# Dealing the modulation groups of a two-layer diffusion backbone out anew over the chunks of layer 0

## The chip, the cores and the metric

The kernel runs on one core of a Trainium2 chip. The metric is the device time of one execution in microseconds (us). The core has these engines: PE multiplies matrices, DVE (VectorE) and ACT (ScalarE) work on tensors, POOL (GpSimd) does a little of that too, and SP only issues transfers. Each engine works through its own queue in program order and waits on semaphores for the others.

## The reference, cut to what matters

Two layers work on 256 latent tokens and 256 context tokens of 1024 channels. Every layer begins with a modulation: a vector per stream (c for the latent tokens, c_ctx for the context) goes through silu and a 1024 x 6144 weight, and gives six vectors of 1024 (shift, scale and gate of the mixer, shift, scale and gate of the feed-forward part).

```python
def adaln(cvec, w, b):
    m = jax.nn.silu(cvec) @ w + b
    return [t[..., None, :] for t in jnp.split(m, 6, axis=-1)]

for l in range(DEPTH):
    sh1, sc1, gt1, sh2, sc2, gt2 = adaln(c, w_ada[l], b_ada[l])
    csh1, csc1, cgt1, csh2, csc2, cgt2 = adaln(c_ctx, w_ada[l], b_ada[l])
    hx = modulate(rms_norm(x, g_mix[l]), sh1, sc1)      # the same for ctx
    ...                                                 # four branches, merged, @ w_out
    x = x + gt1 * mixer_output(...)
    x = x + gt2 * conv_ffn(modulate(rms_norm(x, g_ffn[l]), sh2, sc2), w_up[l], ..., w_down[l])
```

In the last layer the context only gives keys and values, so of its modulation only shift and scale of the mixer are needed there.

## The kernel before

**Chunks.** All weights stream through in 244 chunks, 122 to a layer, each 128 x 1024 to 128 x 1408 numbers. The stages of a layer and their first chunk: in 0, fn 18, sc 26, at 34, cf 46, out 54, up0 62, dn0 84, up1 92, dn1 114. Layer 0 has both streams (512 columns for a matmul), layer 1 has one (256 columns). Numbers such as "chunk 72" below are of layer 0.

**Three products.** For every chunk ACT copies the raw weights to `w_hi` (`head`, L881), DVE subtracts to get `w_lo` (`rest`, L1165), and PE multiplies three times (L480 to L482). Both run AHEAD = 3 chunks in front of PE: in its step n the DVE first makes the rest of chunk n+3, then waits for PE to finish chunk n, reads its result out of PSUM (in the stages out and dn this is the residual, L1529, two instructions of 256 columns; in the up stages L1555 and L1558 for an even chunk and L1565 for an odd one), and last does `ada_behind`. PE begins a chunk when its rest is there and the chunk four before it has been read out.

**Lead.** At the start of out, up0 and dn0/dn1 PE computes the first three chunks together (`lead`), so it needs the rests of all three before it begins; their results come almost together.

**Norm.** After stage out and after dn1 comes a norm, and PE has nothing to multiply until its first channels are there. Its chain: DVE reads out the last chunk (of out: chunk 61, in two halves, one for each stream), ACT squares the half, PE sums, ACT takes the root, DVE the reciprocal (L1239) and a diagonal, PE spreads it, DVE scales (L1269), ACT adds the shift, DVE gives the remainder (L1280). During stage out DVE also adds the squares of the earlier chunks (`add_square`, L1234).

**Modulation groups.** The 12 groups of 1024 modulation values (layer 0: 0 to 5, layer 1: 6 to 11, in the order of the reference) take eight chunks of `w_ada` each. Groups 1 and 0 are done by PE at the start. For the other ten `ADA_START[g]` is the chunk of layer 0 behind which the first of eight steps is done, `ada_step`: DVE multiplies a 128 x 1024 piece of `w_ada` with a column of the silu and adds it to `ada_sum` (L1186; the first step of a group L1184). Groups 0 to 7 have two vectors (c and c_ctx) and take two such instructions a step; I call them double. Groups 8 to 11 are single. After the eighth step DVE folds `ada_sum` to 128 x 32 for each vector (L1193). `REDUCE` gives the chunk in front of which PE does the last reduction (`reduce_in_front`, L522), for which it waits for the folds; DVE reads it one step earlier in its own count (`read_mod`, L1205, L1214), since PE reduces behind chunk n-1 and in front of n.

**Transfers.** SP loads chunks and `w_ada` pieces into four shared slots of `raw`, in one fixed order (`FILLS`), each when the entry four before it has been used.

Of the kernel before, what the change touches and what calls it, by code (L numbers as in the profile page):

```python
# [15 lines left out]
ALU = mybir.AluOpType  # L16
ACT = mybir.ActivationFunctionType
AX = mybir.AxisListType
# [28 lines left out]
START, SIZE, LEN = {}, [], {}  # L47
# [10 lines left out]


ADA_START = {2: START["in"] + 2, 3: START["at"] + 3, 4: START["at"] + 11}  # L60
for _g in range(5, 12):
    ADA_START[_g] = START["up0"] + 8 * (_g - 5)
ORDER = [1, 0] + sorted(ADA_START, key=ADA_START.get)
POS = {_g: _p for _p, _g in enumerate(ORDER)}
REDUCE = {START["out"] + 3 if _g == 4 else ADA_START[_g] + 10: _g for _g in ADA_START}
ADA_AT = {ADA_START[_g] + _k: 8 * _g + _k for _g in ADA_START for _k in range(8)}
assert len(ADA_AT) == DEPTH * ADA_L - ADA_A and max(REDUCE) < PER_LAYER - 1
ADA_LOADS = [(0, 1), (1, 1)] + [(_i, 2) for _i in range(2, ADA_A, 2)]
# [13 lines left out]
def ada_vectors(a):  # L82


    return 2 if a < ADA_L or a % ADA_L < 16 else 1
# [69 lines left out]
def program(nc, io):  # L155
    ctx = ExitStack()
    with ctx:
# [23 lines left out]
        ada_sum = place("ada_sum", [2, KD * P])  # L181
# [31 lines left out]
        ada_part = place("ada_part", [2, P * KD // 32])  # L213
# [47 lines left out]
        csil_done, nsink_done, mod_done, gsc_done = map(sem, ("csil_done", "nsink_done", "mod_done", "gsc_done"))  # L261
# [895 lines left out]
        def _(dve):  # L1157
# [13 lines left out]
            def ada_step(a):  # L1171

                p, g, kk = PLACE[("ada", a)], a // 8, a % 8
                dve.wait_ge(raw_full[p % SLOTS], 16 * (p // SLOTS + 1))
                if kk == 0 and g == 2:
                    dve.wait_ge(reduced, 2)
                elif kk == 0:
                    dve.wait_ge(folded, POS[g] - 2)
                else:
                    dve.wait_ge(ada_acc, ADA_STEPS[a] - ada_vectors(a))  # L1180
                for vv in range(ada_vectors(a)):
                    w, dst, c = raw[:, p % SLOTS, 0:KD * P], ada_sum[:, vv, :], csil[:, kk, vv:vv + 1]
                    if kk == 0:
                        op = dve.tensor_scalar(dst, w, c, None, ALU.mult)  # L1184
                    else:
                        op = dve.scalar_tensor_tensor(dst, w, c, dst, ALU.mult, ALU.add)  # L1186
                    op.then_inc(ada_acc, 1)
                if kk == KD - 1:

                    dve.wait_ge(ada_acc, ADA_STEPS[a])  # L1190
                    dve.wait_ge(reduced, POS[g])
                    for vv in range(ada_vectors(a)):
                        op = dve.tensor_reduce(ada_part[:, vv, :], ada_sum[:, vv, :].rearrange("p (b k) -> p b k", k=32),  # L1193
                                               AX.X, ALU.add, apply_transpose=True)
                    op.then_inc(folded, 1)

            def read_mod(g, bank):

                dve.wait_ge(reduced, POS[g] + 1)
                layer, c0 = g // 6, KD * (g % 6)  # L1200
                b = VEC["b_ada"] + KD * g
                vs = ada_vectors(8 * g)
                ps = bank[:, 0:2 * KD].rearrange("p (c v) -> p v c" if g < 2 else "p (v c) -> p v c", v=2)
                for vv in range(vs):
                    op = dve.tensor_tensor(mod[:, layer, c0:c0 + KD, vv], ps[:, vv, :], vec[:, b:b + KD], ALU.add)  # L1205
                op.then_inc(mod_done, 1)
                if g % 6 in (1, 4):

                    dve.wait_ge(mod_done, POS[g] + 1)
                    which = g % 6 // 3  # L1210
                    gv = VEC["g_mix" if which == 0 else "g_ffn"] + KD * layer
                    for vv in range(2):
                        if vv < vs:
                            op = dve.scalar_tensor_tensor(gsc[:, which, vv, :], mod[:, layer, c0:c0 + KD, vv],  # L1214
                                                          1.0, vec[:, gv:gv + KD], ALU.add, ALU.mult)
                    op.then_inc(gsc_done, 1)

            def ada_behind(st):

                if st.i is None:  # L1220
                    if st.n + 1 in REDUCE:
                        read_mod(REDUCE[st.n + 1], psB[(st.n + 1) % 2])
                    if st.n in ADA_AT:
                        ada_step(ADA_AT[st.n])

# [26 lines left out]
            def norm(layer, which):  # L1252
                r = 2 * layer + which
                if r:
                    inverse_root(r, 0)
                dve.wait_ge(gsc_done, r + 1)
                for s in range(norm_streams(r)):
                    h0 = 16 * r + KD * s
                    cols = slice(s * SEQ, (s + 1) * SEQ)
                    dve.wait_ge(spread, normed(r, s))  # L1260
                    for kk in range(KD + 1):
                        if r == 2 and s == 1 and kk in SPLIT_IN_NORM:
                            if kk:
                                query(Step(PER_LAYER + SPLIT_IN_NORM[kk] - 1, SPLIT_IN_NORM[kk] - 1))
                            rest(Step(PER_LAYER + SPLIT_IN_NORM[kk], SPLIT_IN_NORM[kk]), SIZE[AHEAD])
                        if kk < KD:
                            if kk >= 2:
                                dve.wait_ge(h_rest, h0 + kk - 1)
                            dve.scalar_tensor_tensor(tmp[kk % 2][:, cols], X[:, kk, cols],  # L1269
                                                     gsc[:, which, s, kk:kk + 1], spread_bank[s][:, cols],  # L1270
                                                     ALU.mult, ALU.mult).then_inc(ht, 1)
                        if kk == 1 and s == 0:
                            if r == 0:
                                read_mod(ORDER[1], psB[1 + ORDER[1]])
                            if norm_streams(r) > 1:
                                inverse_root(r, 1)
                        if kk >= 1:
                            c = kk - 1
                            dve.wait_ge(h_head, h0 + c + 1)
                            dve.scalar_tensor_tensor(h_lo[:, c, cols], tmp[c % 2][:, cols],  # L1280
                                                     mod[:, layer, 24 * which + c, s:s + 1],
                                                     h_hi[:, c, cols].bitcast(F32), ALU.add, ALU.subtract)\
                                .then_inc(h_rest, 1)
# [8 lines left out]
            for ahead in range(AHEAD):  # L1292
                dve.wait_ge(ada_pe, first_free(2 * SLOTS + ahead))
                if ahead == AHEAD - 1:
                    g = ORDER[1]
# [4 lines left out]
            for layer in range(DEPTH):  # L1300
# [6 lines left out]
                for idx in range(LEN["in"]):  # L1307
                    st = Step(n0 + idx, idx)
# [41 lines left out]
                    if 6 <= idx < 11:  # L1350
# [3 lines left out]
                        r = 15 * layer + 3 * j  # L1354
# [104 lines left out]
                for idx in range(LEN["at"]):  # L1459
                    st = Step(m0 + idx, idx)  # L1460
# [243 lines left out]
```

## Time and profile before

| | us |
|---|---|
| median of 3 runs | 1343.0 (1340.77 to 1345.43) |
| profiled execution, own time | 1344.04 |
| its span | 1342.3 |
| PE busy | 1287.8 (96%) |
| DVE busy | 883.2 (66%) |
| ACT busy | 555.6 (41%) |
| POOL busy | 289.8 (22%) |

The span runs from the first to the last instruction of the profiled execution, and the time is 1.7 us longer than it. PE's granted clock was 0.985 of full speed on average. An engine's busy share says little of where it is late: what counts here are the few places at which PE stands still, and what it waits for there.

### The profile page before, as it was taken

The numbers are of one execution on the slowest core, as the hardware profiler recorded it, in microseconds if no ns is written. First come the engines' busy times: TensorE is split into PE (matmuls) and PEld (weight loads), VectorE is DVE, ScalarE is ACT, GpSimd is POOL, SyncE is SP. The second block draws the span as 40 slices with busy tenths as digits, with TensorE's granted clock in tenths as the row PEclk, the third lists the DMA queues.
The fourth block names the chain that finished last, engine by engine and source line by source line (L and its number), as shares of the span: only waits on it lengthen the run. The fifth ranks groups of instructions, "written<-read, shape, count | busy, mean of one in ns | idle before, by whom it ended". The sixth has DMA issues, their size and how long they took to land.

```text
span 1342.3 us, 19885 instructions
## 1 busy us (share of the span) xinstructions
PE 1287.8 (96%) x7677; PEld 1101.3 (82%) x7677; DVE 883.2 (66%) x1193; ACT 555.6 (41%) x868; POOL 289.8 (22%) x246
## 2 busy tenths in 40 slices
PE   7999999999999999999999999989999998999997
PEld 1788877777788788787788888889888898999997
DVE  1686378753689568997656664576677466764654
ACT  2322345654333234333123332344566464653543
POOL 0000499310223100112001110002782230120210
PEclk9899999999999999999999999989999999999999
DMA  9364221222546323667456663425333554564560
GB/s 371 112 188 153 81 76 61 71 63 63 161 141 247 107 82 121 202 195 223 140 166 193 196 204 122 151 79 173 119 118 98 169 174 142 172 214 147 181 211 32
DMA packets 51234, 198.75 MB, mean 148 GB/s; under 512 B 5584, under 2 KB 6864, under 8 KB 50896
## 3 DMA queue, kind: packets, MB, share of 16 engines
q1 hardware_dynamic: 51152, 197.62, 45.2%
q8 instruction: 56, 0.92, 0.3%
q14 instruction: 26, 0.21, 0.1%
HBM read 196.55 MB, written 1.05 MB: 147 GB/s over the span
## 4 chain that ended last, share of the span: by engine, by line
PE 78%; DVE 13%; issue 4%; ACT 3%; DMA 1%; SPq 0%; DVEq 0%; ACTq 0%
PE psA L480 22%; PE psA L482 22%; PE psA L481 22%; DVE w_lo L1165 3%; DVE ada_sum L1186 2%; DVE acc L1374 2%; PE psB L480 2%; PE psB L481 2%; PE psB L482 2%; ACT w_hi L881 1%; DMA ada_first<-w_ada 1%; PE psA L501 1%; DVE small L1387 1%; PE psB L726 1%; PE psB L633 1%
## 5 line engine op out<-in xcount | busy, mean ns | idle before, releaser
L480 PE MATMUL psA<-h_hi,w_hi 128*128 128x256 f32 (+1 forms) x1568 | 529.8, 338 | 9.5 <-DVE h_lo L1280 6.4
L481 PE MATMUL psA<-h_lo,w_hi 128*128 128x256 f32 (+1 forms) x1568 | 523.4, 334 | 0.0
L482 PE MATMUL psA<-h_hi,w_lo 128*128 128x256 f32 (+1 forms) x1568 | 523.3, 334 | 0.0
L881 ACT ACTIVATE w_hi<-raw 128x1024 fp32r<-128x1024 f32 (+2 forms) x244 | 277.1, 1138 | 340.3 <-PE psA L482 243.8
L1165 DVE TENSOR_TENSOR w_lo<-raw,w_hi 128x1024 fp32r<-128x1024 f32 (+2 forms) x244 | 332.7, 1364 | 126.7 <-ACT w_hi L881 126.5
L480 PEld LDWEIGHTS psA<-h_hi,w_hi 128*128 128x128 f32 x1568 | 302.6, 193 | 38.5 <-issue 7.6
L481 PEld LDWEIGHTS psA<-h_lo,w_hi 128*128 128x128 f32 x1568 | 302.7, 193 | 28.1 <-issue 0.5
L482 PEld LDWEIGHTS psA<-h_hi,w_lo 128*128 128x128 f32 x1568 | 302.2, 193 | 28.0
L469 POOL TENSOR_TENSOR hid_lo<-sig,hid_hi 128x512 f32 (+3 forms) x44 | 67.7, 1538 | 486.7 <-ACT hid_hi L1129 486.7
L1186 DVE SCALAR_TENSOR_TENSOR ada_sum<-raw,csil,ada_sum 128x1024 f32<-128x1024 f32 x112 | 159.3, 1452 | 0.0
L480 PE MATMUL psA<-hid_hi,w_hi 128*128 128x256 f32 (+1 forms) x352 | 117.8, 335 | 3.5 <-DVE sig L1565 2.1
L482 PE MATMUL psA<-hid_hi,w_lo 128*128 128x256 f32 (+1 forms) x352 | 117.3, 333 | 0.0
L481 PE MATMUL psA<-hid_lo,w_hi 128*128 128x256 f32 (+1 forms) x352 | 117.3, 333 | 0.0
L1529 DVE SCALAR_TENSOR_TENSOR X<-psA,mod,X 128x256 f32<-128x256 f32 x55 | 25.1, 479 | 85.7 <-PE psA L482 85.7
L480 PEld LDWEIGHTS psA<-hid_hi,w_hi 128*128 128x128 f32 x352 | 66.9, 190 | 11.0 <-DVE w_lo L1165 4.1
L444 POOL TENSOR_TENSOR acc<-acc,sqb 128x512 f32<-128x512 f32 (+1 forms) x60 | 74.5, 1241 | 5.0
L482 PEld LDWEIGHTS psA<-hid_hi,w_lo 128*128 128x128 f32 x352 | 66.9, 190 | 6.5
L481 PEld LDWEIGHTS psA<-hid_lo,w_hi 128*128 128x128 f32 x352 | 66.9, 190 | 6.4
L450 POOL TENSOR_TENSOR X<-X,tmp 128x512 f32<-128x512 f32 (+1 forms) x28 | 43.3, 1555 | 125.2 <-DVE tmp L1479 76.3
L1140 ACT ACTIVATE tmp<-psA,vec 128x512 f32<-128x512 f32 (+1 forms) x44 | 29.5, 671 | 96.2 <-PE psA L482 96.2
L1555 DVE SCALAR_TENSOR_TENSOR tmp<-psA,vec,tmp 128x510 f32<-128x510 f32 (+1 forms) x44 | 27.0, 613 | 62.1 <-ACT tmp L1140 62.0
L480 PE MATMUL psB<-y_hi,w_hi 128*128 128x512 f32 (+1 forms) x128 | 46.6, 364 | 13.4 <-issue 7.3
(170 smaller groups left out, 1453.9 us busy)
## 6 DMA issues: line engine op xcount, KB each, us to landing
raw<-w_up SPq DMA_DIRECT2D x88, 512.0 KB, 4.2
raw<-w_ada SPq DMA_DIRECT2D x80, 512.0 KB, 3.6
raw<-w_dn SPq DMA_DIRECT2D x32, 704.0 KB, 5.2
raw<-w_in SPq DMA_DIRECT2D x36, 512.0 KB, 4.3
raw<-w_at SPq DMA_DIRECT2D x24, 512.0 KB, 3.5
raw<-w_fn SPq DMA_DIRECT2D x16, 640.0 KB, 3.9
raw<-w_sc SPq DMA_DIRECT2D x16, 640.0 KB, 3.9
raw<-w_cf SPq DMA_DIRECT2D x16, 640.0 KB, 4.0
```

The lines of the kernel that those rows point to most:

```text
L444: pool.tensor_tensor(dst, dst, part, ALU.add).then_inc(tap_pool, 1)
L450: pool.tensor_tensor(dst, dst, src[:, 0:T], ALU.add).then_inc(m_sum, 1)
L469: pool.tensor_tensor(dst, sig[b][:, 0:T], src.bitcast(F32), ALU.subtract)\
L480: pe.matmul(out, w0, hi, start=first, stop=False)
L481: pe.matmul(out, w0, lo, start=False, stop=False)
L482: return pe.matmul(out, w1, hi, start=False, stop=last)
L881: act.activation(w_hi[:, s, 0:tiles * P], raw[:, r, 0:tiles * P], ACT.Copy).then_inc(head_done, 1)
L1140: act.activation(tmp[b][:, 0:T], psA[st.slot][:, 0:T], ACT.Identity, bias=Vd("ffn_b", st.up(p0 + pair, 2)), scale=Vd("ffn_w", st.up(3 * (p ...
L1165: dve.tensor_tensor(w_lo[:, s, 0:tiles * P], raw[:, r, 0:tiles * P], w_hi[:, s, 0:tiles * P].bitcast(F32), ALU.subtract).then_inc(rest_don ...
L1186: op = dve.scalar_tensor_tensor(dst, w, c, dst, ALU.mult, ALU.add)
L1374: op = dve.scalar_tensor_tensor(dst, src, w, dst, ALU.mult, ALU.add)
L1555: dve.scalar_tensor_tensor(t3[:, :, 1:SEQ], p3[:, :, 0:SEQ - 1], Vd("ffn_w", st.up(w, 6)), t3[:, :, 1:SEQ], ALU.mult, ALU.add).then_inc(cv, 1)
```

## The change

It alters at which chunks the groups 5 to 11 are done, and it separates the two folds of a double group.

| group | vectors | chunks before | reduced before | chunks after | reduced after |
|---|---|---|---|---|---|
| 2, 3, 4 | 2 | 2-9, 37-44, 45-52 | 12, 47, 57 | the same | the same |
| 5 | 2 | 62-69 | 72 | 53-60 | 65 |
| 6 | 2 | 70-77 | 80 | 84-91 | 94 |
| 7 | 2 | 78-85 | 88 | 108-115 | 118 |
| 8 | 1 | 86-93 | 96 | 62-69 | 72 |
| 9 | 1 | 94-101 | 104 | 70-77 | 80 |
| 10 | 1 | 102-109 | 112 | 92-99 | 102 |
| 11 | 1 | 110-117 | 120 | 100-107 | 110 |

So after the change no group is worked on behind chunks 61, 78 to 83 and 116 to 121. The first fold of a double group stays in the step of its eighth product. The second is done one step later, after that step's result has been read out and before that step's product, if there is one (`ADA_END`). The waits of the norms for their scale (`gsc_done`) get the counts of the new order (`GAINS`).

```diff
-for _g in range(5, 12):
-    ADA_START[_g] = START["up0"] + 8 * (_g - 5)
+for _g, _n in [(5, START["cf"] + 7), (8, START["up0"]), (9, START["up0"] + 8), (6, START["dn0"]), (10, START["up1"]),
+               (11, START["up1"] + 8), (7, START["up1"] + 16)]:
+    ADA_START[_g] = _n
 ORDER = [1, 0] + sorted(ADA_START, key=ADA_START.get)
 POS = {_g: _p for _p, _g in enumerate(ORDER)}
-REDUCE = {START["out"] + 3 if _g == 4 else ADA_START[_g] + 10: _g for _g in ADA_START}
+REDUCE = {{4: START["out"] + 3, 5: START["up0"] + 3}.get(_g, ADA_START[_g] + 10): _g for _g in ADA_START}
+ADA_END = {ADA_START[_g] + 8: _g for _g in ADA_START}
+GAINS = {_r: 1 + sum(ADA_START[_g] <= ADA_START[_h] for _g in (4, 7, 10)) for _r, _h in [(1, 4), (2, 7), (3, 10)]}
+GAINS[0], GAINS[3] = 1, max(GAINS[2], GAINS[3])
...
                     dve.wait_ge(ada_acc, ADA_STEPS[a])
                     dve.wait_ge(reduced, POS[g])
-                    for vv in range(ada_vectors(a)):
-                        op = dve.tensor_reduce(ada_part[:, vv, :], ada_sum[:, vv, :].rearrange("p (b k) -> p b k", k=32),
-                                               AX.X, ALU.add, apply_transpose=True)
+                    ada_fold(g, 0)
+
+            def ada_fold(g, vv):
+
+                op = dve.tensor_reduce(ada_part[:, vv, :], ada_sum[:, vv, :].rearrange("p (b k) -> p b k", k=32),
+                                       AX.X, ALU.add, apply_transpose=True)
+                if vv == ada_vectors(8 * g) - 1:
                     op.then_inc(folded, 1)
...
                     if st.n + 1 in REDUCE:
                         read_mod(REDUCE[st.n + 1], psB[(st.n + 1) % 2])
+                    if st.n in ADA_END and ada_vectors(8 * ADA_END[st.n]) == 2:
+                        ada_fold(ADA_END[st.n], 1)
                     if st.n in ADA_AT:
                         ada_step(ADA_AT[st.n])
...
-                dve.wait_ge(gsc_done, r + 1)
+                dve.wait_ge(gsc_done, GAINS[r])
```

## Rows read from the trace of the kernel before

**Rows 1.** The page: totals of the engines; loads of `w_ada`, us to landing.
```profile
PE 1287.8 (96%) x7677; PEld 1101.3 (82%) x7677; DVE 883.2 (66%) x1193; ACT 555.6 (41%) x868; POOL 289.8 (22%) x246
...
raw<-w_ada SPq DMA_DIRECT2D x80, 512.0 KB, 3.6
```

**Rows 2.** Timeline of PE: start us, us, what; in brackets the idle before, and its releaser.
```profile
447.35 0.47 PE L480 MATMUL psA<-mg_hi,w_hi 128*128 128x512 f32 x1 [1.62 <-DVE w_lo L1165]
...
557.40 0.26 PE L522 MATMUL psB<-ada_part,mat 128*32 128x16 f32 x8 [3.04 <-DVE ada_part L1193]
...
626.51 0.47 PE L480 MATMUL psA<-hid_hi,w_hi 128*128 128x512 f32 x1 [1.30 <-DVE w_lo L1165]
...
658.44 0.26 PE L522 MATMUL psB<-ada_part,mat 128*32 128x16 f32 x8 [1.73 <-DVE ada_part L1193]
```

**Rows 3.** Windows: length, busy us of PE, PEld, DVE, ACT, POOL, granted clock, DMA share, GB/s.
```profile
554.38:564.95 10.57, 7.55 (x33) 6.12 (x34) 10.50 (x14) 3.37 (x4) 1.23 (x1) 0.84 0.58 179
603.02:608.90 5.88, 5.88 (x33) 4.86 (x34) 5.88 (x8) 1.69 (x2) 1.63 (x1) 1.00 0.67 214
570.38:575.83 5.45, 5.45 (x25) 4.52 (x25) 5.45 (x5) 1.70 (x2) 1.49 (x1) 1.00 0.68 230
...
491.93:515.55 23.62, 20.96 (x163) 20.82 (x164) 17.04 (x40) 9.59 (x20) 0.00 (x0) 0.93 0.08 24
1131.99:1147.59 15.60, 12.19 (x80) 11.76 (x81) 9.46 (x21) 5.68 (x12) 0.00 (x0) 0.78 0.18 55
...
625.22:649.25 24.03, 22.74 (x100) 18.88 (x101) 7.83 (x8) 3.19 (x3) 1.61 (x1) 1.00 0.34 105
809.80:832.59 22.79, 22.70 (x100) 18.86 (x101) 5.08 (x6) 3.18 (x3) 1.60 (x1) 1.00 0.32 103
```

**Rows 4.** Timeline of DVE at the start of stage out.
```profile
462.64 0.88 DVE L1529 SCALAR_TENSOR_TENSOR X<-psA,mod,x_in 128x256 f32<-128x256 f32 x2 [10.13 <-PE psA L482]
463.79 1.23 DVE L1165 TENSOR_TENSOR w_lo<-raw,w_hi 128x1024 fp32r<-128x1024 f32 x1 [0.28 <-ACT w_hi L881]
464.93 0.87 DVE L1529 SCALAR_TENSOR_TENSOR X<-psA,mod,x_in 128x256 f32<-128x256 f32 x2
...
466.85 0.68 DVE L1234 TENSOR_TENSOR sqa<-sqa,sqb 128x512 f32<-128x512 f32 x1
467.45 0.87 DVE L1529 SCALAR_TENSOR_TENSOR X<-psA,mod,x_in 128x256 f32<-128x256 f32 x2
468.24 0.23 DVE L1205 TENSOR_TENSOR mod<-psB,vec 128x8 f32<-128x8 f32 x2
...
468.66 1.22 DVE L1165 TENSOR_TENSOR w_lo<-raw,w_hi 128x1024 fp32r<-128x1024 f32 x1
```

**Rows 5.** Timeline of DVE at the start of dn0, double group 7 ending.
```profile
647.91 0.88 DVE L1529 SCALAR_TENSOR_TENSOR X<-psA,mod,X 128x256 f32<-128x256 f32 x2 [16.20 <-PE psA L482]
648.70 2.47 DVE L1186 SCALAR_TENSOR_TENSOR ada_sum<-raw,csil,ada_sum 128x1024 f32<-128x1024 f32 x2
651.09 1.62 DVE L1165 TENSOR_TENSOR w_lo<-raw,w_hi 128x1408 fp32r<-128x1408 f32 x1
...
655.92 2.37 DVE L1193 TRANSPOSE_TENSOR_REDUCE ada_part<-ada_sum 128x32 f32<-128x1024 f32 x2
658.22 1.58 DVE L1165 TENSOR_TENSOR w_lo<-raw,w_hi 128x1408 fp32r<-128x1408 f32 x1
```

**Rows 6.** Timeline of DVE into two norms (the last one of layer 1).
```profile
491.95 0.48 DVE L1529 SCALAR_TENSOR_TENSOR X<-psB,mod,x_in 128x256 f32<-128x256 f32 x1 [2.38 <-PE psB L482]
493.06 0.17 DVE L1239 RECIPROCAL root_col<-root_col 128x2 f32<-128x2 f32 x1 [0.63 <-ACT root_col L913]
...
1134.00 0.17 DVE L1239 RECIPROCAL root_col<-root_col 128x2 f32<-128x2 f32 x1 [1.50 <-ACT root_col L913]
```

**Rows 7.** Timeline of POOL, its first instruction after stage cf.
```profile
521.92 1.47 POOL L469 TENSOR_TENSOR hid_lo<-sig,hid_hi 128x512 f32 x1 [72.36 <-ACT hid_hi L1129]
```

**Rows 8.** DVE's products in 515.5:554, as a group: busy, mean ns, idle before.
```profile
L1186 DVE SCALAR_TENSOR_TENSOR ada_sum<-raw,csil,ada_sum 128x1024 f32<-128x1024 f32 x14 | 21.4, 1572 | 0.0
```

## The prediction

> **What bounds the kernel now.** I read the engines' totals first, then PE's waits, then the timeline around each. PE is busy for 1287.8 us of the span of 1342.3 [rows 1]. So this change can only win or lose where PE stands still, and DVE's share of 66% decides nothing by itself. In layer 0, behind the start, PE stops for DVE's modulation work at four places [rows 2]. At 447.35 it had been idle for 1.62 us, before stage out, for the rest of the third chunk of the lead. At 557.40 it had waited 3.04 us in front of chunk 72 for the folds of group 5. At 626.51 it had waited 1.30 us before dn0, again for a rest. At 658.44 it had waited 1.73 us in front of chunk 88 for the folds of group 7. The reader should see that the product and not only the fold is what makes DVE late: in 515.5:554 DVE did 14 products of 1572 ns mean and had no idle time before any of them [rows 8]. Two other stops, the norms, are a chain that begins with DVE's read-out of the stage's last chunk [rows 3, 6]. There DVE's lateness is PE's idle time, microsecond for microsecond.
>
> **Durations of DVE's pieces**, start to start (instructions overlap a little). In stage out: rest 1.14 us (463.79 to 464.93), squares added 0.60 (466.85 to 467.45), read-out of a chunk 0.79 (467.45 to 468.24), group 4's values read 0.42 (468.24 to 468.66) [rows 4]. A double product is 2.39 us (648.70 to 651.09), two folds are 2.30 (655.92 to 658.22), so one is 1.15. The rest of a wide chunk is 1.62 long, and with the overlap of 0.08 that its neighbours show I count 1.54 [rows 5]. All product prices are taken from DVE alone. Where POOL works beside it the mean is 1572 ns instead of half of 2.39 [rows 8].
>
> **1. Second fold of group 4 goes behind the read-out of chunk 53: 1.15 us won.** Before, both folds stand ahead of the rest of chunk 56, for which PE waited 1.62 us [rows 2]. One fold moves behind it, so the wait is 1.15 shorter. What it is moved before: group 5's first product and the last rest of the merged stream. The latter is needed as the eighth input of three chunks that PE multiplies for some 16 us, so it has cover of over ten. DVE then has 10.13 us idle before chunk 54 [rows 4]. The folds of groups 2 and 3 are split too. I cost them at nothing: step 45 reads out its chunk 1.15 sooner and folds for 1.15 after it, so what PE gets in front of chunk 47 is ready when it was; the rotary work of stage in covers group 2's.
>
> **2. Group 5 goes into stage out: 7.0 us lost.** This is the main term. Before, DVE's queue from the read-out of chunk 54 (462.64) to that of chunk 61 (491.95) had gaps, and the last read-out waited 2.38 us for PE [rows 4, 6]. Now I add up everything in DVE's queue from 462.64 on. Seven double products (behind chunks 54 to 60), 7 x 2.39 = 16.7. Seven rests (of chunks 58 to 64), 7 x 1.14 = 8.0. Eight read-outs, 8 x 0.79 = 6.3. Six additions of squares, 6 x 0.60 = 3.6. Group 4's values, 0.4. Two folds, 2.3, and 0.1 for their waits. The sum is 37.4 us, which ends at 500.0. PE is done with chunk 61 at 491.95 as before: the rests come 1.7 us or more ahead of it by the same adding up (rest of 60 at 476.6 against a need at 480.7, rest of 61 at 481.6 against 486.2). The norm's reciprocal was at 493.06 [rows 6]. DVE is free for it at 500.0. From the end of the first half's read-out (498.6) the chain over ACT and PE takes 1.50 us, the idle time in front of the same reciprocal in layer 1 [rows 6], which gives 500.1, the same. So 500.1 - 493.06 = 7.0 us. The point from which it costs: without the products the queue holds 37.4 - 16.7 = 20.7 us, and 493.06 is 30.4 us behind 462.64, so a pair would have to take under (30.4 - 20.7) / 7 = 1.4 us. Above that each 0.1 us of the pair costs 0.7.
>
> Bounds of this term. From above: if the products there ran at the mean of 1572 ns, a pair is 3.14 and 7 x 0.75 = 5.3 us more are lost. I don't take it, since POOL has nothing to do between stage cf and 521.92 [rows 7]. From below: no mechanism in the rows makes the pair shorter than 2.39. The pieces' transfers: one chunk and one piece in every 4.9 us is about 213 GB/s, no more than the 214 and 230 that windows of up0 show [rows 3], and a piece, which SP can issue when the piece two steps before has been used, has one whole step and the next read-out, over 6 us, until its use, against 3.6 to landing [rows 1]. The chunk loads that SP issues between the pieces have as long. So nothing is added for them. On the port: all products of DVE have two SBUF inputs. The Trainium skill, "SBUF — State Buffer", section "Who interferes with whom", says that such an instruction contends with a GpSimd one that reads SBUF, and that the second to come is blocked until the other is done. By that rule the move takes seven pairs away from POOL's instructions and into a silent stage; by the rule and by the row a pair is 2.39 there, and with POOL in it the term would be 12.3.
>
> PE's clock after the longer pause. The norm had a mean of 0.93 in 23.62 us, so (1 - 0.93) x 23.62 / 0.5 = 3.3 us at 1.2 GHz. The one norm that restarts on a single stream had 0.78 in 15.60 us, or 6.9 us at that level [rows 3]. Both ends for the longer pause: 0 and, with twice the stretch, 1.7 us more. I take 0, since one stretch is charged already. The Trainium skill, "TensorE: Matmul & The Clock Gate", Part 1, says that throttled is the default state and activity releases it; by that a pause that has already cost the clock costs none further, and the term stays 7.0, where the layer 1 row would make it 8.7.
>
> **3. Stage up0 gets single groups: 4.7 us won.** Chunk 72 took 10.57 us; one with a reduction and no wait takes 5.88 (603.02 to 608.90) and one without 5.45 [rows 3]. The difference of 10.57 - 5.88 = 4.7 is the wait of 3.04 and the clock behind it: (1 - 0.84) x 10.57 / 0.5 = 3.4 us at half speed, 1.7 lost. After the change chunk 65 has group 5's reduction, whose folds are done before the norm, and 72 and 80 those of single groups whose DVE steps need 1.2 us less than before. The number of reductions, 0.43 us each, stays the same.
>
> **4. The lead of dn0 wins 1.2, the lead of dn1 loses 1.2.** dn0's took 24.03 us behind double products and dn1's 22.79 behind single ones [rows 3]. Chunks 78 to 83 now have none, while 108 to 113 are double. The two swap, and cancel.
>
> **5. Group 7's folds leave dn0: 1.8 won.** PE's 1.73 and the start behind it go. Group 6 that comes to 84 to 91 is folded in steps 91 and 92, and reduced in front of 94, over 5 us later.
>
> **6. Group 7's folds come to dn1, the second a step later: 6.2 lost.** The places are the same relative to the stage, but in dn0 both folds stood in the step of chunk 85. From the read-out of chunk 84 (647.91) to PE's running dry is 8.8 us (658.44 - 1.73 - 647.91) [rows 2, 5]. In dn1 DVE has, from chunk 114's read-out: 0.79 + 2.39 (product), 1.54 (rest) + 0.79 + 2.39 + 1.15 (first fold), then 1.54 (rest) + 0.60 (squares) + 0.79 + 1.15 (second fold) = 13.1, and 0.2 to PE's start. PE waits 13.3 - 8.8 = 4.5 us, instead of 1.73. A wait of 3.04 cost 1.7 of clock [rows 2, 3], one of 1.73 none; 4.5 lies beyond the first, so I add 1.7. Its bound from below is 0. Behind the waiting PE stands only chunk 118; DVE's later steps have no modulation and catch up before the next norm.
>
> **Sum.** -1.15 - 4.7 - 1.2 - 1.8 + 7.0 + 1.2 + 6.2 = +5.6 us. Against the profiled execution's 1344.04 that is 1349.6. That execution lies 1.0 above the median of 1343.0, so the prediction for the median is 1348.6.
>
> **The rivals.** I count a difference of over 0.3%, 4.0 us, as faster or slower; a measurement of this kernel tells less than that hardly from no change.
> - Stage out hides group 5 (it ends on the other side). Its mechanism: the norm's reciprocal stays at 493, because DVE catches up. For it speaks that a step with a pair is 1.14 + 0.60 + 0.79 + 2.39 = 4.9 us and PE's chunk 5.45. Against it speaks that the lead hands DVE three chunks at once: eight steps have only the 29.3 us from 462.64 to 491.95. It decides from a pair of 1.4 us down. Then the sum is 5.6 - 7.0 = -1.4, or 1341.6. Chance 0.10.
> - The wait in dn1 is small, since the fold is ready when PE comes. For it: before, PE waited only 1.73 at that place. Against: the rest, squares and read-out that now lie between the folds. The time is 5.6 - 6.2 = -0.6, or 1342.4. Chance 0.10; together with the first -7.6, or 1335.4, chance 0.05.
> - The norm restarts with a longer stretch at half clock, as layer 1's did: 1350.3. Chance 0.15.
> - Products in stage out are as dear as beside POOL, or wait for their transfers: 5.6 + 5.3, or 1353.9. Chance 0.08.
> - My forecast, 1348.6, with its own range 1346.8 (no clock loss at chunk 118) to 1350.3: chance 0.52.
>
> **How the numbers follow.** Slower by over 0.3% means above 1347.0. Of my forecast's 0.52 about 0.44 lie there, and 0.15 + 0.08 of the dearer cases: 0.67. The two small cases and the rest of mine are no change, 0.26. Both small together are faster, 0.07 with what I may have missed. The range that holds 8 in 10 reaches from 1342.4 to 1352.5.
>
> **What the profile should show.** DVE without idle time from about 461.5 to 499, and its reciprocal of the norm some 8 us behind PE's last product of stage out, instead of 1.1. PE in front of chunk 72 without a wait. The third rest of dn1's lead 1 us after PE wants it. In front of chunk 118 a wait of PE for L1193 of 4.5 us and a granted clock below 1 behind it. I am wrong if DVE shows gaps in stage out, or if the second fold of group 7 comes before the rest of chunk 119.

## The result, and the profile after

The change makes the kernel slower: 1352.07 us (median of 5 runs, 1349.95 to 1354.01) against 1344.49 (5 runs of the kernel before on the same chip), a ratio of 1.0058 (of the changed kernel's time to that of the kernel before) with a 95% interval of 1.0044 to 1.0071. That is 7.6 us by the medians and 7.8 by the ratio, where 5.6 were forecast. The profiled executions took 1351.27 and 1344.04; their spans differ by 7.2 us. The profiled execution of the changed kernel had a mean granted clock of 0.982, its other four 0.978 to 0.981. One execution of e1 (2132.52 us) and one of e2 (3113.51 us) lie far outside the rest and are left out of what follows.

Line numbers move by 4 to 10 in the changed kernel (L1186, the product, is L1190 there, the fold L1200, the rest L1169, the residual L1539, the norm's reciprocal L1249). First the page's totals, the places at which PE restarts (timeline of PE, with the idle time before), and then windows with the columns of [rows 3], in this order: the norm with up0's lead, chunk 72, chunk 118, dn0's lead.

```profile
PE 1290.2 (96%) x7677; PEld 1104.0 (82%) x7677; DVE 877.5 (65%) x1193; ACT 554.7 (41%) x868; POOL 288.3 (21%) x246
```

```profile
446.59 0.47 PE L484 MATMUL psA<-mg_hi,w_hi 128*128 128x512 f32 x1 [0.49 <-DVE w_lo L1169]
...
497.48 1.02 PE L581 MATMUL psB<-mat,sqa 128*128 128x1 f32 x4 [6.34 <-DVE sqa L1244]
...
500.47 1.22 PE L589 MATMUL psB<-sqb,mat 128*128 128x128 f32 x4 [1.07 <-DVE sqb L1252]
...
504.74 0.56 PE L484 MATMUL psA<-h_hi,w_hi 128*128 128x256 f32 x1 [1.55 <-DVE h_lo L1290]
...
810.74 0.47 PE L484 MATMUL psA<-hid_hi,w_hi 128*128 128x512 f32 x1 [1.35 <-DVE w_lo L1169]
...
845.57 0.26 PE L526 MATMUL psB<-ada_part,mat 128*32 128x16 f32 x4 [4.64 <-DVE ada_part L1200]
```

```profile
491.16:523.27 32.11, 23.16 (x164) 23.02 (x165) 24.71 (x50) 12.16 (x24) 0.00 (x0) 0.79 0.23 78
562.50:568.35 5.85, 5.85 (x33) 4.85 (x34) 4.20 (x4) 1.58 (x2) 1.28 (x1) 1.00 0.75 218
840.95:855.10 14.15, 9.53 (x42) 7.78 (x43) 9.89 (x16) 2.53 (x3) 0.00 (x0) 0.88 0.49 160
628.61:651.05 22.44, 22.44 (x100) 18.59 (x100) 3.65 (x5) 3.18 (x3) 1.29 (x1) 1.00 0.16 53
```

Read against [rows 2, 3]: the wait ahead of stage out is 1.13 us shorter, the norm with up0's lead takes 32.11 us instead of 23.62, chunk 72 takes 5.85 instead of 10.57, dn0's lead 22.44 instead of 24.03, and PE waits 4.64 us in front of chunk 118, which takes 14.15 us in all. PE's total rose by 2.4 us with the same matmuls: it spent longer at the lower clock. DVE's total fell, and the kernel is slower.

DVE's queue through stage out, from its timeline. The lines left out repeat the same four (product, rest, squares, read-out), and once stand the four small instructions of group 4's values:

```profile
461.87 0.88 DVE L1539 SCALAR_TENSOR_TENSOR X<-psA,mod,x_in 128x256 f32<-128x256 f32 x2 [10.03 <-PE psA L486]
462.66 2.47 DVE L1190 SCALAR_TENSOR_TENSOR ada_sum<-raw,csil,ada_sum 128x1024 f32<-128x1024 f32 x2
465.06 1.21 DVE L1169 TENSOR_TENSOR w_lo<-raw,w_hi 128x1024 fp32r<-128x1024 f32 x1
...
494.47 1.25 DVE L1200 TRANSPOSE_TENSOR_REDUCE ada_part<-ada_sum 128x32 f32<-128x1024 f32 x1
495.64 1.18 DVE L1169 TENSOR_TENSOR w_lo<-raw,w_hi 128x1024 fp32r<-128x1024 f32 x1
496.75 0.68 DVE L1244 TENSOR_TENSOR sqa<-sqa,sqb 128x512 f32<-128x512 f32 x1
497.34 0.47 DVE L1539 SCALAR_TENSOR_TENSOR X<-psA,mod,x_in 128x256 f32<-128x256 f32 x1
497.74 0.47 DVE L1539 SCALAR_TENSOR_TENSOR X<-psB,mod,x_in 128x256 f32<-128x256 f32 x1
498.13 1.23 DVE L1200 TRANSPOSE_TENSOR_REDUCE ada_part<-ada_sum 128x32 f32<-128x1024 f32 x1
499.73 0.17 DVE L1249 RECIPROCAL root_col<-root_col 128x2 f32<-128x2 f32 x1 [0.37 <-ACT root_col L917]
```

There is no idle time from 461.87 to the end of the last fold at 499.36. The queue is 37.5 us long; 37.4 had been added up. The grouped view of DVE in 462:500 gives the price of the products; below it stands POOL's first instruction after stage cf:

```profile
L1190 DVE SCALAR_TENSOR_TENSOR ada_sum<-raw,csil,ada_sum 128x1024 f32<-128x1024 f32 x14 | 17.3, 1277 | 0.0
...
528.97 1.47 POOL L473 TENSOR_TENSOR hid_lo<-sig,hid_hi 128x512 f32 x1 [80.17 <-ACT hid_hi L1133]
```

1277 ns for one against the 1572 of [rows 8]: with POOL silent, for 80.17 us up to 528.97, they are at the low price.

Laid side by side, the differences of the two executions are: lead of out -1.13, norm and up0's lead +8.5, chunk 72 with the reduction that went to 65 -4.3, dn0's lead -1.6, chunk 88 -2.2, dn1's lead +1.3, chunk 118 with the reduction that went from 120 +6.25. Their sum is +6.8; 0.5 more arose ahead of chunk 4, where the two programs do the same work. The start is not the same length in every execution: DVE's rest of chunk 10 comes between 1.4 us earlier (e1) and 2.1 later (e9) than in the kernel before.

### The profile page after: what moved, and what is told of

Read it like the earlier page. It is cut to its first block, busy times and chain, and to the rows that moved or that the text cites. A ratio compares the mean times of both kernels' runs of the same rounds, so it can differ in the third digit from the quotient of the medians.

```text
span 1349.5 us, 19884 instructions
## 1 busy us (share of the span) xinstructions
PE 1290.2 (96%) x7677; PEld 1104.0 (82%) x7677; DVE 877.5 (65%) x1193; ACT 554.7 (41%) x868; POOL 288.3 (21%) x246
## 4 chain that ended last, share of the span: by engine, by line
PE 78%; DVE 13%; issue 3%; ACT 3%; DMA 1%; SPq 0%; DVEq 0%; ACTq 0%
PE psA L484 22%; PE psA L486 22%; PE psA L485 22%; DVE w_lo L1169 3%; DVE ada_sum L1190 3%; PE psB L484 2%; DVE acc L1384 2%; PE psB L486 2%; PE psB L485 2%; ACT w_hi L885 1%; DMA ada_first<-w_ada 1%; PE psA L505 1%; DVE small L1397 1%; PE psB L730 1%; PE psB L718 1%
## 5 line engine op out<-in xcount | busy, mean ns | idle before, releaser
L1169 DVE TENSOR_TENSOR w_lo<-raw,w_hi 128x1024 fp32r<-128x1024 f32 (+2 forms) x244 | 333.4, 1367 | 127.5 <-ACT w_hi L885 127.4
L1190 DVE SCALAR_TENSOR_TENSOR ada_sum<-raw,csil,ada_sum 128x1024 f32<-128x1024 f32 x112 | 152.0, 1388 | 0.0
L1539 DVE SCALAR_TENSOR_TENSOR X<-psA,mod,X 128x256 f32<-128x256 f32 x55 | 25.1, 478 | 86.5 <-PE psA L486 86.5
```

The source lines that it names most:

```text
L1169: dve.tensor_tensor(w_lo[:, s, 0:tiles * P], raw[:, r, 0:tiles * P], w_hi[:, s, 0:tiles * P].bitcast(F32), ALU.subtract).then_inc(rest_don ...
```

## Experiments

The times are medians; each ratio is against runs of the kernel before on the same chip (its medians there: 1343.92 for e1 to e4, 1345.11 for e5 to e7, 1345.18 for e8 and e9, 1343.88 for e10 and e11). "Under the changed kernel" compares medians, 1352.07 for the changed one. That one belongs to another series, so the difference of the ratios, of which its own is 1.0058, is the safer comparison, and stands beside it where the two differ.

**e1: a single group in stage out.** Groups 5 and 8 exchanged, the same number of pieces and transfers in every stage.

```diff
-for _g, _n in [(5, START["cf"] + 7), (8, START["up0"]), (9, START["up0"] + 8), (6, START["dn0"]), (10, START["up1"]),
+for _g, _n in [(8, START["cf"] + 7), (5, START["up0"]), (9, START["up0"] + 8), (6, START["dn0"]), (10, START["up1"]),
...
-REDUCE = {{4: START["out"] + 3, 5: START["up0"] + 3}.get(_g, ADA_START[_g] + 10): _g for _g in ADA_START}
+REDUCE = {{4: START["out"] + 3, 8: START["up0"] + 3, 5: START["up0"] + 12}.get(_g, ADA_START[_g] + 10): _g for _g in ADA_START}
```

> The changed kernel with groups 8 and 5 exchanged: single group 8 behind chunks 53 to 60 (reduced in front of 65), double group 5 behind 62 to 69 and reduced only in front of 74. The number of transfers in stage out stays the same. Theory (DVE's queue sets the start of the norm): seven single products of 1.2 us and one fold make the queue from chunk 54's read-out to 61's about 28 us, under the 30.4 to the reciprocal, so the norm starts as in the kernel before, and the time is 8.5 us under the changed kernel's, near 1343.5 (about 1 below the kernel before). Rival (the pieces' transfers or SP's order make stage out late): the norm stays as late as in the changed kernel, and the time is that of the changed kernel, 1352.

Measured: 1344.79 us, ratio 1.0007 (0.9995 to 1.0019), so 7.3 us under the changed kernel by medians and 6.9 by ratios, where 8.5 had been expected. The norm and up0's lead take 24.56 us (489.30:513.86), 7.55 less than in the changed kernel and 0.94 more than before. In DVE's timeline the read-outs wait for PE again, and the norm's reciprocal comes 1.2 us behind the end of chunk 61 (489.30):

```profile
483.57 0.88 DVE L1539 SCALAR_TENSOR_TENSOR X<-psA,mod,x_in 128x256 f32<-128x256 f32 x2 [1.34 <-PE psA L486]
...
490.52 0.17 DVE L1249 RECIPROCAL root_col<-root_col 128x2 f32<-128x2 f32 x1 [0.72 <-ACT root_col L917]
```

The rival, transfers, falls: their number is the same. The norm was late by DVE's second vector alone.

**e2: group 7 reduced two chunks later**, the rest as changed.

```diff
-REDUCE = {{4: START["out"] + 3, 5: START["up0"] + 3}.get(_g, ADA_START[_g] + 10): _g for _g in ADA_START}
+REDUCE = {{4: START["out"] + 3, 5: START["up0"] + 3, 7: START["dn1"] + 6}.get(_g, ADA_START[_g] + 10): _g for _g in ADA_START}
```

> The changed kernel with group 7 reduced in front of chunk 120 and not of 118. Theory (PE only waits for the second fold because it asks for it too early): the wait of 4.6 us and the 1.7 of half clock behind it vanish, chunk 118 takes 7.5 us instead of 14.15, and nothing comes up later: 6.2 us under the changed kernel, near 1346. Rival (DVE is late in dn1 for rests as well): PE would wait for L1169 at chunk 118 or 119 instead, and gain under 3 us.

Measured: 1345.59, ratio 1.0013 (1.0002 to 1.0024), 6.5 us under the changed kernel by medians and 6.0 by ratios, where 6.2 had been expected. In its windows chunk 118 takes 7.48 us and chunk 120, with the reduction, 7.92; both at full clock:

```profile
839.09:846.57 7.48, 7.48 (x34) 6.19 (x34) 7.48 (x11) 1.97 (x3) 0.00 (x0) 1.00 0.56 177
854.05:861.97 7.92, 7.92 (x43) 6.55 (x44) 3.00 (x8) 1.58 (x2) 0.00 (x0) 1.00 0.21 66
```

The rival, late rests, falls: PE waits for none of them there.

**e3: the folds together again**, in the changed order.

```diff
-                    ada_fold(g, 0)
+                    for vv in range(ada_vectors(a)):
+                        ada_fold(g, vv)
...
-                    if st.n in ADA_END and ada_vectors(8 * ADA_END[st.n]) == 2:
-                        ada_fold(ADA_END[st.n], 1)
```

> The changed kernel with both folds of a double group in the step of its last product, the order of groups as changed. Theory: stage out's lead begins 1.15 us later again, the norm's reciprocal comes 1.15 later (the first half's read-out now has both folds of group 5 ahead of it), and the wait in front of chunk 118 shrinks from 4.6 to 1.7 with no half clock behind it, 4.6 us less: 2.3 us under the changed kernel in all. Rival (separating the folds is a gain at the norm and at 118 alike): slower than the changed kernel by 2 us or more.

Measured: 1351.75, ratio 1.0058 (1.0041 to 1.0075). The time does not tell it from the changed kernel, and the 2.3 us forecast did not appear. The profile shows the terms, though. The lead of out is 1.13 us later, norm and lead take 33.52 instead of 32.11, and the wait in front of chunk 118 is 1.73, with no low clock behind it, so that this chunk takes 9.70 us (841.40:851.10) instead of 14.15:

```profile
491.94:525.46 33.52, 23.45 (x164) 23.31 (x165) 24.70 (x50) 12.23 (x25) 0.00 (x0) 0.80 0.24 77
...
844.83 0.25 PE L526 MATMUL psB<-ada_part,mat 128*32 128x16 f32 x7 [1.73 <-DVE ada_part L1201]
```

These sum to -1.9 us; the next norm gave 0.8 back in its traced execution. The rival of a loss of 2 us fell as well.

**e4: only the folds separate**, the order as before (the diff is against the changed kernel).

```diff
-for _g, _n in [(5, START["cf"] + 7), (8, START["up0"]), (9, START["up0"] + 8), (6, START["dn0"]), (10, START["up1"]),
-               (11, START["up1"] + 8), (7, START["up1"] + 16)]:
+for _g, _n in [(_h, START["up0"] + 8 * (_h - 5)) for _h in range(5, 12)]:
...
-REDUCE = {{4: START["out"] + 3, 5: START["up0"] + 3}.get(_g, ADA_START[_g] + 10): _g for _g in ADA_START}
+REDUCE = {{4: START["out"] + 3}.get(_g, ADA_START[_g] + 10): _g for _g in ADA_START}
```

> The kernel before with its order of groups, only the second fold one step later. Theory: 1.15 us won at stage out's lead; in front of chunk 72 the second fold now has a rest and a read-out ahead of it, 2.4 us more wait; in front of chunk 88 2.3 us more wait (4.1) and 1.7 of half clock: 5.2 us over the kernel before, near 1349. Rival (the separate folds alone do no harm, all the loss is the order's): the time of the kernel before or 1 us less.

Measured: 1351.61, ratio 1.0052 (1.0032 to 1.0072), 7 us of loss from an edit of which no instruction is new; 5.2 had been expected. Its timeline of PE and its window of chunk 88:

```profile
559.27 0.26 PE L525 MATMUL psB<-ada_part,mat 128*32 128x16 f32 x4 [4.59 <-DVE ada_part L1199]
...
662.41 0.30 PE L525 MATMUL psB<-ada_part,mat 128*32 128x16 f32 x7 [4.05 <-DVE ada_part L1199]
```

```profile
658.38:673.09 14.71, 10.68 (x42) 8.63 (x43) 10.13 (x15) 2.75 (x2) 0.00 (x0) 0.77 0.71 231
```

In front of 72 PE waits 1.55 us more than before, in front of 88 2.32 more, and there the clock stays low for (1 - 0.77) x 14.71 / 0.5 = 6.8 us, where nothing of it was lost before: chunk 88 costs 5.0 more. Chunk 72 costs 1.3 more and the lead of out 1.13 less. What the forecast lacked is in the two norms with their leads, 0.85 and 1.1 us longer than in the kernel before, each with 6.8 us at 1.2 GHz instead of 3.4.

**e5: the kernel before with two reductions later**, and nothing else.

```diff
-REDUCE = {START["out"] + 3 if _g == 4 else ADA_START[_g] + 10: _g for _g in ADA_START}
+REDUCE = {{4: START["out"] + 3, 5: START["up0"] + 12, 7: START["dn0"] + 6}.get(_g, ADA_START[_g] + 10): _g for _g in ADA_START}
```

> The kernel before, its order of groups and its folds unchanged, with only two reductions later: group 5's in front of chunk 74 (not 72), group 7's in front of 90 (not 88). Theory (what up0 and dn0 lost was only that PE asked too early): chunk 72 takes 5.45 instead of 10.57 us, chunk 88 7.48 instead of 9.70, chunks 74 and 90 0.43 more each: 6.5 us under the kernel before, near 1337.5. Rival (DVE stays late after double groups, and the waits reappear in front of 74 and 90, or of rests): under 3 us gained.

Measured: 1343.93, ratio 0.999 (0.9979 to 1.0002): nothing won that is clear of noise. The waits at 72 and 88 did vanish (5.44 us for chunk 72). What chunk 88 gave, 2.2 less 0.4 for the reduction that moved, is within this interval. PE's timeline and the window of dn0's lead show where the first went:

```profile
624.73 0.77 PE L480 MATMUL psA<-hid_hi,w_hi 128*128 128x512 f32 x1 [3.54 <-DVE w_lo L1165]
```

```profile
621.19:648.92 27.73, 24.20 (x94) 19.80 (x95) 8.72 (x7) 2.76 (x4) 1.59 (x1) 0.88 0.34 112
```

The window ends with the first of the lead's three chunks; the other two take 1.4 us more, which makes 29.1 us instead of 24.03 [rows 3], with 3.54 us of wait in it and half clock behind that. With double products in all of up0 DVE has no slack: its timeline shows no idle time from 599.82 to 624.88. PE's wait in front of chunk 72 had been the time in which it caught up; without it, DVE's lateness arrived at the next place that needs it. So the rival held, and the 4.7 us are won only together with single groups in up0. This says that term 3 of the prediction is the order's, not the reduction's.

**e6: a better order.** Group 8 behind 53 to 60, 5 behind 62 to 69 (reduced in front of 74), 9, 6, 7, 10, 11 behind 70, 84, 92, 100 and 108; folds separate.

```diff
-for _g, _n in [(5, START["cf"] + 7), (8, START["up0"]), (9, START["up0"] + 8), (6, START["dn0"]), (10, START["up1"]),
-               (11, START["up1"] + 8), (7, START["up1"] + 16)]:
+for _g, _n in [(8, START["cf"] + 7), (5, START["up0"]), (9, START["up0"] + 8), (6, START["dn0"]), (7, START["up1"]),
+               (10, START["up1"] + 8), (11, START["up1"] + 16)]:
...
-REDUCE = {{4: START["out"] + 3, 5: START["up0"] + 3}.get(_g, ADA_START[_g] + 10): _g for _g in ADA_START}
+REDUCE = {{4: START["out"] + 3, 8: START["up0"] + 3, 5: START["up0"] + 12}.get(_g, ADA_START[_g] + 10): _g for _g in ADA_START}
```

> The changed kernel with group 8 (single) behind 53 to 60, 5 behind 62 to 69 and reduced in front of 74, 9 behind 70 to 77, 6 behind 84 to 91, 7 behind 92 to 99, 10 behind 100 to 107, 11 behind 108 to 115. Theory: it keeps the changed kernel's gains (1.15 at stage out's lead, 4.7 in front of chunk 72, 1.2 to 1.6 at dn0's lead, 2.2 at chunk 88) and has neither loss: no late norm, no wait in front of 118, and dn1's lead behind single products as before. 9 us under the kernel before, near 1335. Rival (double products are dear wherever they are put): within 3 us of the kernel before.

Measured: 1336.26, ratio 0.9928 (0.9914 to 0.9942): 8.8 us under the kernel before by its median there and 9.7 by the ratio, 9 were forecast. In its profile chunk 72 takes 5.44 us and dn0's lead 22.44, no wait of PE for modulation between stage out and layer 1.

**e7 and e8: PE kept at work in the norm's pause.** The changed kernel; in e7 only 24 added matmuls ahead of the sums, in e8 28, 4 and 5. The edit of e8:

```diff
+                def keep(n):
+                    if r == 1:
+                        for _ in range(n):
+                            pe.matmul(psB[2][:, :], w_hi[:, 61 % SLOTS, 0:P], mg_hi[:, 0, :], start=True, stop=True)
+                keep(28)
                 mean_square(r, 0)
+                keep(4)
                 spread_inverse(r, 0)
                 if norm_streams(r) > 1:
                     mean_square(r, 1)
+                    keep(5)
```

> The changed kernel, with 24 matmuls of 512 columns more on PE between chunk 61 and the norm's sums, into a bank that nothing reads. Theory (the longer pause costs beyond DVE's 7.4 us because the norm's own small matmuls run at 1.2 GHz): PE is kept at work for 5.2 of its 6.3 us of waiting, the clock stays at 2.4 GHz, from the reciprocal to the first matmul of up0's lead it takes 3.8 us as before and not 5.0, and the lead loses its half clock too: 1.2 to 2.8 us under the changed kernel. Rival (the 1.2 us are no matter of the clock): no gain, or a loss as the added matmuls delay the norm's sums.

> The changed kernel with 28 added matmuls of 512 columns behind chunk 61, 4 behind the norm's first sums and 5 behind its second, all into a bank that nothing reads. 24 alone left PE idle for 0.9 us before the sums and for longer stretches in the chain behind, and the clock fell there. Theory: with the pauses filled the clock does not fall at this norm, the reciprocal to the first matmul of up0's lead takes 3.8 us and the lead runs at 2.4 GHz throughout, 16.4 to 17 us and not 18.6: 2.5 to 3 us under the changed kernel in the profile. Rival (the chain's length has nothing to do with the clock): the gap from the reciprocal to the lead stays 4.8 to 5.0 us.

Measured: e7 1350.78, ratio 1.0037 (1.0021 to 1.0053); e8 1350.79, ratio 1.0047 (1.0029 to 1.0065). By medians both are 1.3 us under the changed kernel, by ratios 2.8 (e7) and 1.5 (e8); the spread of the runs does not clear either (e7's eight lie between 1346.64 and 1353.75). By the profile e7 gains 0.6 us at this place (31.53, granted clock 0.89), since the clock still fell in the chain behind. In e8's profiled execution it did not fall at all; the windows of norm and lead, and of the lead alone:

```profile
490.29:519.48 29.19, 28.56 (x201) 26.01 (x201) 24.66 (x50) 12.17 (x24) 0.00 (x0) 1.00 0.23 76
502.24:519.48 17.24, 17.24 (x144) 17.24 (x145) 13.87 (x30) 7.98 (x15) 0.00 (x0) 1.00 0.05 14
```

29.19 instead of 32.11: 2.9 us. From the reciprocal to the lead's first matmul it took 3.8 us as before, and 5.0 in the changed kernel; the lead took 17.24 instead of 18.5, and the reciprocal itself came 0.4 us sooner behind chunk 61. This is one execution: its mean clock was 0.988, that of the other three of e8 0.983 to 0.984, and they took 1349.67 to 1352.81 us against its 1347.21. So e8 shows what the fall costs, and not that these matmuls keep it away every time.

**e9, e10, e11: the better order with the folds together**, alone (e9, and again as e11) and with PE kept at work in the two norms of both streams (e10). The hunks of the order and of the folds are those of e6 and e3; what e10 adds:

```diff
+                def keep(n, cols):
+                    if r in (1, 2):
+                        for _ in range(n):
+                            pe.matmul(psB[2][:, 0:cols], M("ident"), M("pos", cols), start=True, stop=True)
                 mean_square(r, 0)
+                keep(1, 512)
                 spread_inverse(r, 0)
                 if norm_streams(r) > 1:
                     mean_square(r, 1)
+                    keep(2, 352)
```

> The kernel with the better order (group 8 behind 53 to 60, 5 behind 62 to 69 and reduced in front of 74, 9, 6, 7, 10, 11 behind), but both folds of a double group in one step. Theory: the separate folds gain 1.15 us at stage out's lead and nothing elsewhere in this order, so this one is 1.1 us slower than with the folds separate, near 1337.4, all of it at chunk 54. Rival (separate folds matter elsewhere too): over 3 us slower.

> The better order with the folds together, and at the two norms of both streams PE gets one added matmul of 512 columns behind the first sums and two of 352 behind the second (float32, a bank that nothing reads). Theory: the clock does not fall at these norms, each lead loses its 1.6 us of half clock: 3 us under the same kernel without them, near 1333. Rival (the clock falls at some other moment of the chain all the same, or the added matmuls hold up the spread): within 1 us of it.

> The better order with the folds together once more, beside the one with filled pauses, on the same chip: 9 us under the kernel before, 1336, and 3 us above the filled one if the theory holds.

Measured: e9 1336.17, ratio 0.9934 (0.9917 to 0.9952), no slower than e6. The 1.13 us at stage out's lead were lost as expected, but its norm and lead took 23.55 us at a clock of 0.93, and e6's 24.58 at 0.86. In these two profiles, e6's first, what the separate folds gained at one place was lost at the next:

```profile
492.45:517.03 24.58, 21.95 (x163) 21.77 (x164) 17.03 (x40) 9.92 (x21) 0.00 (x0) 0.86 0.12 41
```

```profile
490.92:514.47 23.55, 20.92 (x163) 20.74 (x164) 17.03 (x40) 9.92 (x21) 0.00 (x0) 0.93 0.13 44
```

e11 1337.63, ratio 0.995 (0.9933 to 0.9966). e10, beside it, 1333.99, ratio 0.9921 (0.9903 to 0.9938), 3.6 us under e11 and 9.9 under the kernel before. Its two norms, beside e11's below them:

```profile
492.25:514.51 22.26, 21.89 (x169) 20.28 (x170) 17.03 (x40) 9.91 (x21) 0.00 (x0) 1.00 0.10 34
861.78:875.62 13.84, 13.12 (x97) 11.55 (x98) 11.11 (x26) 6.04 (x13) 1.95 (x2) 1.00 0.00 1
```

```profile
493.70:517.44 23.74, 21.11 (x163) 20.93 (x164) 17.04 (x40) 9.91 (x21) 0.00 (x0) 0.93 0.12 43
864.72:880.90 16.18, 13.21 (x91) 13.07 (x92) 11.60 (x27) 6.53 (x14) 1.95 (x2) 0.79 0.08 19
```

22.26 against 23.74 and 13.84 against 16.18: 3.8 us by three added matmuls in each. The times agree: all five executions of e10 (1331.68 to 1334.23) lie under all six of e11 (1335.80 to 1339.04), with mean clocks of 0.988 to 0.990 against 0.984 to 0.985. e10 is the fastest version here.

How much there is to gain differs from one execution to the next. The norm behind dn1, with its lead, in the kernel before, in the changed kernel and in e1, which have the same work there as the changed one:

```profile
870.85:885.98 15.13, 12.15 (x91) 12.01 (x92) 11.61 (x27) 6.53 (x14) 1.95 (x2) 0.89 0.07 16
877.97:893.27 15.30, 12.32 (x91) 12.19 (x92) 11.60 (x27) 6.53 (x14) 1.95 (x2) 0.89 0.08 22
868.70:886.41 17.71, 14.73 (x91) 14.59 (x92) 11.61 (x27) 6.53 (x14) 1.95 (x2) 0.71 0.09 30
```

By the clock that is 3.3, 3.4 and 10.3 us at 1.2 GHz, and 6.8 in e11. Against the kernel before, e10's 13.84 is 1.3 us shorter at this place, not 2.3.

## Why the prediction was right, and which term was too small

The direction, its mechanism and all six terms are in the trace. The forecast for the median, 1348.6, is 3.5 us under the measured 1352.07. Of this 1.5 are the kernel before itself, whose median rose from 1343.0 (three executions) to 1344.49 (five); 2.0 are the change. The time lies above the forecast's own range (to 1350.3) and just inside the wide one (to 1352.5). By the prediction's own steps:

1. Separate folds ahead of stage out: -1.15 forecast, -1.13 measured. e4, e6 and e9 show something beside it: in the profiles with separate folds and no late norm (e1, e4, e6) the next norm had a clock of 0.86, in those with the folds together (the kernel before, e5, e9, e11) 0.93, and 0.8 to 1.0 us came back there. That the folds are the cause is not shown. There is one profile of each, and at the norm behind dn1 the clock was low for 3.4 us in the changed kernel and for 10.3 in e1 with the same work there.
2. Group 5 in stage out: 7.0 forecast, 8.5 measured. The queue was right (37.4 forecast, 37.5 measured), and the reciprocal came 8.6 us behind PE's last product instead of 1.1. The term that was mis-sized is the clock after the longer pause, taken as 0 with 1.7 as its other end. The stretch had 13.5 us at 1.2 GHz, (1 - 0.79) x 32.11 / 0.5, instead of 3.3. Cut at the lead's first matmul, before and after (two windows each, chain and lead), with PE's sums and spread of the chain before:

```profile
491.93:496.86 4.93, 2.27 (x20) 2.13 (x20) 3.16 (x11) 1.62 (x5) 0.00 (x0) 0.99 0.00 0
496.86:515.55 18.69, 18.69 (x144) 18.69 (x145) 13.88 (x30) 7.97 (x15) 0.00 (x0) 0.91 0.10 30
...
491.16:504.74 13.58, 4.64 (x20) 4.50 (x21) 10.83 (x21) 4.18 (x9) 0.00 (x0) 0.60 0.41 144
504.74:523.27 18.53, 18.53 (x144) 18.53 (x145) 13.88 (x30) 7.98 (x15) 0.00 (x0) 0.92 0.09 31
...
491.75 0.50 PE L577 MATMUL psB<-mat,sqa 128*128 128x1 f32 x4
...
493.80 0.71 PE L585 MATMUL psB<-sqb,mat 128*128 128x128 f32 x4 [1.10 <-DVE sqb L1242]
```

   Before, the clock was up in the chain (0.99) and fell as the lead began. Now it was low for (1 - 0.60) x 13.58 / 0.5 = 10.9 of the 13.58 us ahead of the lead, so it had fallen while PE stood idle, and all of the chain ran at the low clock: a set of four sums took 1.02 us instead of 0.50, one of four spreads 1.22 instead of 0.71. From the first half's read-out to the reciprocal it took 1.9 us where 1.5 had been counted (e8, with the clock up: 1.5), and from the reciprocal to the lead 5.0 instead of 3.8. The lead was no dearer, 18.5 against 18.7. That is 0.4 + 1.2 - 0.1 = 1.5, the whole difference. e8's profile, in which the clock stayed up, gave 2.9 back: this 1.5 and the loss in the lead that had been there before. The Trainium skill, "TensorE: Matmul & The Clock Gate", Part 1, had been read as a reason for 0. That throttled is the default state agrees with the trace, where PE had nothing to do for 6.34 us and the clock fell within them, but what was concluded from it was wrong: a longer pause moves the fall ahead of the norm's small matmuls, and they lie on the path. e1, with one vector less, takes 7.55 of the 8.5 us away; the other 0.94 went with a low clock of 6.9 us instead of 3.3 in its own norm.
3. Single groups in up0: 4.7 forecast, 4.7 measured at chunk 72. e5 shows that it was not as simple as written: the late reduction alone wins nothing, since DVE's lateness goes on to dn0's lead.
4. The two leads of dn: forecast to cancel at 1.2; -1.6 and +1.3 measured. dn0's lead, now behind no products at all, fell to 22.44, under the 22.79 that dn1's took behind single ones [rows 3].
5. Chunk 88: -1.8 forecast, -2.2 measured, 0.4 of it a reduction that now stands in front of another chunk.
6. Chunk 118: +6.2 forecast, +6.25 measured with the moved reduction; its wait 4.64 us against 4.5. The first signs named were there too: DVE without idle time from 461.87, and a wait of 1.35 us for the third rest of dn1's lead. e2 took the wait at 118 away and won 6.0 by ratios.

The sum of 5.6 was 1.2 us short of the trace's 6.8: 1.5 too little in step 2, and 0.3 the other way in step 4. That is the rival of the longer half clock, which had been given 0.15 and the price of 1.7. The two rivals of small costs fall in the trace (the late reciprocal, the wait of 4.64) and by e1 and e2. That of dear products falls too: they took 1277 ns, and DVE did not wait for a transfer. On the port between DVE and POOL, the rule of the Trainium skill that the prediction drew on ("SBUF — State Buffer", section "Who interferes with whom") agrees with the trace, with 1277 ns where POOL was silent and 1572 beside it.

What stays open is why e3's gain in the profile does not show in its median. Executions differ by more than this gain, in the length of the start and in how long the clock stays low at a norm, and only one of each is profiled.

## What to carry to other kernels

Side work on an engine with a queue of its own is not free where that engine's queue ends in the chain of a barrier (here a norm): add up the whole queue from the last point at which it was idle, and remember that a lead that hands over several chunks at once has already used up the slack of the stage. Work that is merely early or late (a fold, a reduction) should be asked for as late as its reader allows, but taking away a wait only helps if the engine behind it has caught up by the next place that waits (e5). And a pause on PE is dearer than its length: three matmuls of no use in the chain of each of two norms bought 1.3 to 2.3 us apiece (e10), while 24 ahead of the sums alone (e7) did not keep the clock up.

## What the runs showed of the hardware

- A longer pause of PE cost more than its length. With 6.34 us without work the clock fell to 1.2 GHz inside the pause and stayed there through the norm's small matmuls and into the lead, 13.5 us in all; after the short pauses of the kernel before (none over 1.6 us) it fell as the lead began, for 3.3 us.
- Waits of 3.04, 4.05, 4.59 and 4.64 us in front of a reduction, and one of 3.54 in front of a lead, went with a stretch at 1.2 GHz; one of 1.73 did not, in the kernel before and in e3. The stretches behind 4.05 (e4) and 3.54 (e5) were 6.8 us long, those behind 3.04, 4.59 (e4, chunk 72) and 4.64 were 3.4, so a longer wait is not always the dearer one.
- The same work at the norm behind dn1 had 3.4 us at 1.2 GHz in one execution (the changed kernel) and 10.3 in another (e1), and took 15.30 and 17.71 us.
- An edit that only moved 1.2 us instructions by one step each (e4) cost 7 us.
